# A decoder layer with expert retrieval: fewer v rows in the first chunk's stage, a shorter slot table for the next front

## The reference

```
h = x + W_out[concat(RMSNorm(SBAttn(q, k, v)), ConformerConv(c))]   # [q|k|v|c] = RMSNorm(x) W_in
y = h + PEER(RMSNorm(h))

def peer(xc):                      # one chunk of 128 tokens
    qh = xc @ wq                   # 8 heads, two half keys of 64
    v1, i1 = top_k(qh[..:64] . k1, 16);  v2, i2 = top_k(qh[..64:] . k2, 16)
    cand = v1[:, None] + v2[None, :];    top_s, pos = top_k(cand, 16)
    experts = (i1 * 128 + i2)[pos];      gates = softmax(top_s)
    act = gelu(u_tab[experts] . xc)
    return sum(gates * act * v_tab[experts])
```

## Time and profile before

| | |
|---|---|
| runs | 2912.07 us median, 2910.17 to 2914.2 |
| the profiled execution | span 2910.3 us |
| PE, matmuls | 2591.2 us (89%) |
| DVE | 2110.6 us (73%) |
| POOL | 1986.1 us (68%) |
| ACT | 871.6 us (30%) |
| moved by DMA | 1125 MB, mean 387 GB/s |
| gathers of phase 1 issued | from 337.11 us on |
| first gather of chunk 1 | 572.11 us |

### The profile page before, as it was taken

One profiled execution on the slowest core, in us unless ns is written; L12 is line 12 of the kernel. 1 busy time (PEld: TensorE's weight loads), 2 busy tenths in 40 slices (PEclk: granted clock), 3 DMA queues, 4 the chain that ended last, 5 costly groups with the idle time before them and its releaser, 6 DMA issues.

```text
span 2910.3 us, 29785 instructions
## 1 busy us (share of the span) xinstructions
PE 2591.2 (89%) x7585; PEld 1173.6 (40%) x7585; DVE 2110.6 (73%) x5267; ACT 871.6 (30%) x2022; POOL 1986.1 (68%) x2061
## 2 busy tenths in 40 slices
PE   8999979889978899799979999799988999777777
PEld 4544434433523444244523444244523445222222
DVE  5789758866887678777887778777787757744444
ACT  3223232243213421253214521264214631211111
POOL 1026566677777777777777777777777777777775
PEclk9999999999999999999999999999999999999999
DMA  6239899899999999999999999999999999999999
GB/s 239 96 127 382 331 416 369 316 402 414 419 419 419 413 419 419 409 414 409 416 416 406 411 419 419 419 392 413 419 419 399 385 419 419 415 420 419 420 419 364
DMA packets 321344, 1125.04 MB, mean 387 GB/s; under 512 B 35937, under 2 KB 43641, under 8 KB 321176
## 3 DMA queue, kind: packets, MB, share of 16 engines
q0 software_dynamic: 294912, 1073.87, 91.7%
q1 hardware_dynamic: 26264, 49.27, 4.8%
HBM read 1114.62 MB, written 8.39 MB: 386 GB/s over the span
## 4 chain that ended last, share of the span: by engine, by line
PE 41%; DMA 25%; issue 16%; POOL 12%; DVE 4%; ACT 2%; POOLq 0%; SPq 0%; ACTq 0%; DVEq 0%
PE psum L1614 21%; DMA w_kept<-in_peer_u,experts 12%; DMA ring_v<-in_peer_v,experts 10%; PE psum L514 9%; POOL w_kept L1517 7%; POOL ring_v L1517 5%; PE psum L1038 3%; PE psum L1064 3%; PE psum L1548 2%; DVE w_kept L1933 1%; PE psum L1574 1%; DMA w_kept<-in_peer_v,experts 1%; PE psum L1564 1%; DMA qT_spill<-qT_out 1%; ACT L1751 0%
## 5 line engine op out<-in xcount | busy, mean ns | idle before, releaser
L1614 PE MATMUL psum<-ring_v,diag 128*128 128x512 f32 x3364 | 1619.6, 607 | 252.6 <-DMA ring_v<-in_peer_v,experts 163.9
L1933 DVE CUSTOM_DVE_ANT_0 w_kept<-w_kept,psum 128x1024 f32<-128x1024 f32 x928 | 1125.5, 1217 | 551.2 <-DMA w_kept<-in_peer_u,experts 548.1
L1517 POOL DMA_INDIRECT w_kept<-in_peer_u,experts x928 | 898.2, 968 | 300.1 <-issue 231.4
L1517 POOL DMA_INDIRECT ring_v<-in_peer_v,experts x878 | 847.8, 966 | 327.3 <-issue 234.5
L1614 PEld LDWEIGHTS psum<-ring_v,diag 128*128 128x128 f32 x3364 | 587.1, 191 | 1058.8 <-issue 775.2
L1760 ACT ACTIVATE diag<-ident,weights 128x128 f32<-128x128 f32 x981 | 354.2, 393 | 746.9 <-PE psum L1614 589.9
L1614 PE MATMUL psum<-w_kept,diag 128*128 128x512 f32 x560 | 269.9, 604 | 37.3 <-DMA w_kept<-in_peer_v,experts 23.5
L514 PE MATMUL psum<-w_sb,xnT 128*128 128x512 f32 x640 | 283.5, 599 | 0.8 <-ACT xnT L679 0.8
L466 POOL DMA_INDIRECT w_kept<-in_peer_u,experts x96 | 90.2, 940 | 236.7 <-DVE experts L1324 184.9
L1889 DVE SCALAR_TENSOR_TENSOR acc<-conv_in,taps,acc 128x128 f32<-128x128 f32 x720 | 205.0, 346 | 0.2
L514 PEld LDWEIGHTS psum<-w_sb,xnT 128*128 128x128 f32 x640 | 120.6, 192 | 143.4 <-issue 137.7
(11 more groups left out here) (230 smaller groups left out, 1750.9 us busy)
## 6 DMA issues: line engine op xcount, KB each, us to landing
w_kept<-in_peer_u,experts POOLq DMA_INDIRECT x1024, 9.5
ring_v<-in_peer_v,experts POOLq DMA_INDIRECT x878, 9.5
w_sb<-in_w_in SPq DMA_DIRECT2D x4, 2048.0 KB, 17.6
x_in<-in_x SPq DMA_DIRECT2D x8, 512.0 KB, 6.3
w_kept<-in_w_out SPq DMA_DIRECT2D x1, 4096.0 KB, 14.8
h_res<-in_x SPq DMA_DIRECT2D x8, 512.0 KB, 6.8
w_kept<-in_peer_wq SPq DMA_DIRECT2D x2, 2048.0 KB, 10.6
wo_sb<-in_w_out SPq DMA_DIRECT2D x1, 4096.0 KB, 19.9
```

The source lines that it names most:

```text
L1517: nc.gpsimd.indirect_dma_start(slot(kind, n), None, peer_u[0] if kind == "u" else peer_v[0], bass.IndirectOffsetOnAxis(S.experts[c % 2][:, ...
L1614: last = nc.tensor.matmul(y_ps[:, j * BANK:(j + 1) * BANK], diag[:, e % DIAGS, :], slot("v", n)[:, j * BANK:(j + 1) * BANK], start=e == 0, ...
L1933: nc.vector.tensor_tensor_reduce(out=row, in0=row, in1=hn, scale=1.0, scalar=0.0, op0=ALU.mult, op1=ALU.add, accum_out=dots[:, e:e + 1]).t ...
```

## The change

A class `Plan` computes the front's table from five numbers. Chunks 2 to 7 keep the old table (`LONG`). Chunk 1's front, which runs beside chunk 0's rows, gets a shorter one (`SHORT`): a head every 3 slots, mix in 8, query in 9, the search one slot a step, two of the best-steps in a slot. It comes to 87 slots (`FIRST_SLOTS`), numbered 0 to 86, and chunk 0's stage has that many. In front slots: attention to 29, mix 35 to 42, residual to transposes 43 to 47, query 49 to 57, scores 56, 57, 60, 61, search 58 to 67, candidates 68 to 70, best 71 to 75, look-up 77 to 84, experts 85, gates 86.

v rows get a table of their own, `v_slot`. Chunk 0: 80 rows (`FIRST_ROWS`) from slot 4 on, nearly one a slot, and the 48 others in slots 0 to 47 of chunk 1's stage. Chunk 1's v rows lie evenly from slot 48 of its stage to slot 27 of chunk 2's (128 rows in 108 slots, so that some slots have two), chunk 2's from 28 to slot 19 of chunk 3's (120 slots), and from chunk 3 on it is as before. The stages of chunks 1 to 7 keep 128 slots. `add_h` goes to 2 and 4 slots behind the lag (6 and 8 in chunk 0, 50 and 52 in chunk 1), and `copy_y` / `end_first_y` to the lag. Diagonals are made 3 slots ahead of their row, as before. Of chunk 0's 80 rows every sixth goes aside, 13 instead of 36.

Chunk 0's sum stays in `y_side` and is stored from there. SP's order: the loads of q and conv of chunk f + 1 stand behind the residual's of f, in chunk 1's stage ahead of the store. The diff, cut to its core (each engine's `front` reads the same table; `front_slot` takes the stage's own number of slots):

```diff
-SPREAD = TOPK + 1
-ADD_H = (LAG + 4, LAG + 8)
+BUILD = 3
+FIRST_ROWS = 80
+LAGS = {0: 4, 1: ROWS - FIRST_ROWS, 2: 28}
...
+class Plan:
+    def __init__(self, att_step, mix_slots, query_slots, search_step, per_best):
+        self.step = att_step
+        self.att_end = end = att_step * (HEADS - 1) + ATT_USE
...
+        self.mix, self.mix_slots = end + 6, mix_slots
+        self.h_add, self.h_mean, self.h_norm, self.h_t = (self.mix + mix_slots + n for n in (0, 1, 3, 4))
+        self.query, self.query_slots = self.h_t + 2, query_slots
...
+        first = self.score[1] + 1
+        second = max(self.score[3] + 1, first + (5 if search_step == 1 else 1))
+        self.search = tuple(first + search_step * n for n in range(5)) + tuple(second + search_step * n for n in range(5))
...
+SHORT, LONG = Plan(3, 8, 9, 1, 2), Plan(5, 16, 18, 2, 1)
+FIRST_SLOTS = SHORT.slots
...
+def plan(f):
+    return SHORT if f == 1 else LONG
+
+def slots_of(c):
+    return FIRST_SLOTS if c == 0 else SLOTS
...
-    CAUGHT = ROWS - LAG
-    first_at = {4 + e * (SLOTS - 5) // CAUGHT: e for e in range(CAUGHT)}
-    SIDE = ([row_of(FIRST, e) for e in range(CAUGHT) if e % 3 == 2]
+    STARTS = [sum(slots_of(n) for n in range(c)) for c in range(CHUNKS + 1)]
+    v_slot = []
+    for c in range(CHUNKS):
+        begin, end = STARTS[c] + lag(c), STARTS[c + 1] + lag(c + 1)
+        v_slot += [begin + e * (end - begin) // ROWS for e in range(ROWS)]
+    v_slot[0:ROWS] = [4 + e * (STARTS[1] - 5) // FIRST_ROWS for e in range(FIRST_ROWS)] + [
+        STARTS[1] + n for n in range(ROWS - FIRST_ROWS)]
...
+    SIDE = ([row_of(FIRST, e) for e in range(FIRST_ROWS) if e % 6 == 5]
             + [row_of(TAIL, e) for e in range(ROWS - LAG, ROWS) if e % 3 == 0])
...
+        def load_queries(f):
+            sp.wait_ge(S.z_ready, UNITS * f)
+            sp.dma_start(qT[:, :, :].rearrange("p b t -> p (b t)"), qT_spill[f]).then_inc(S.q_in, 16)
+            sp.wait_ge(S.tapped, TAP_OPS * f)
+            sp.dma_start(conv_in[:, :, :], hT_spill[:, :, f * P:f * P + HALO + P]).then_inc(S.c_in, 16)
...
         def step(c, f):
+            if c is None:
+                return
+            late_rows = lag(c) > LAG + TOPK
+            if late_rows and f is not None and f + 1 < CHUNKS:
+                load_queries(f + 1)
+            if later(c):
+                store(c - 1)
             if f is not None:
-                load_front(f)
-            if c is not None and later(c):
-                store(c - 1)
+                load_residual(f)
+                if not late_rows and f + 1 < CHUNKS:
+                    load_queries(f + 1)
...
-            for s in range(SLOTS):
-                u, v = u_at(c, s), v_at(c, s)
+            for s in range(slots_of(c)):
+                u = u_at(c, s)
                 if u is not None:
                     gather("u", c, u)
-                if v is not None:
+                for v in v_at(c, s):
                     gather("v", *v)
...
-                    if s in ADD_H:
-                        add_h(c, ADD_H.index(s))
+                    for j in range(2):
+                        if s == lag(c) + 2 + 2 * j:
+                            add_h(c, j)
...
-                    if s == LAG and c > FIRST + 1:
+                    if s == lag(c) and c > FIRST + 1:
                         copy_y(c - 1)
...
             if later(f):
                 dve.wait_ge(S.taken, f)
                 dve.wait_ge(S.h_T, 2 * f)
+            if f > 2:
                 dve.wait_ge(y_stored, 16 * (f - 1))
...
+            if n == FIRST_SIDES:
+                dve.wait_ge(y_stored, 16)
...
-            dve.wait_ge(S.taken, FIRST + 2)
...
-                nc.vector.tensor_tensor(y_out[:, at], y_ps[:, at], y_side[:, at], ALU.add).then_inc(y_copied, 1)
+                nc.vector.tensor_tensor(y_side[:, at], y_ps[:, at], y_side[:, at], ALU.add).then_inc(y_copied, 1)
```

More of the change, by code:

```diff
@@ L73 @@
[L73 to L75 removed]
 LOOKS = 8
[L77 to L79 removed]
+MIX_STEPS, QUERY_STEPS = 16, 18
 EARLY_TAPS = range(TAPS - OWN_TAPS)
[L81 to L82 removed]
+class Plan:
+    def __init__(self, att_step, mix_slots, query_slots, search_step, per_best):
+        self.step = att_step
+        self.att_end = end = att_step * (HEADS - 1) + ATT_USE
+        self.conv_t, self.ln_stat, self.ln_scale, self.conv_back = (end + n for n in (-1, 0, 2, 3))
+        self.o_mean, self.o_norm, self.o_t = (end + n for n in (1, 2, 3))
+        self.mix, self.mix_slots = end + 6, mix_slots
+        self.h_add, self.h_mean, self.h_norm, self.h_t = (self.mix + mix_slots + n for n in (0, 1, 3, 4))
+        self.query, self.query_slots = self.h_t + 2, query_slots
+        self.queried = (self.query + (query_slots + 1) // 2 + 1, self.query + query_slots + 1)
+        self.score = (self.queried[0] + 1, self.queried[0] + 2, self.queried[1] + 1, self.queried[1] + 2)
+        first = self.score[1] + 1
+        second = max(self.score[3] + 1, first + (5 if search_step == 1 else 1))
+        self.search = tuple(first + search_step * n for n in range(5)) + tuple(second + search_step * n for n in range(5))
+        self.cand = self.search[-1] + 1
+        self.best = tuple(self.cand + 3 + n // per_best for n in range(10))
+        self.shift = self.split = self.best[-1] + 1
+        self.look = self.split + 1
+        self.experts = self.look + LOOKS
+        self.gates = self.experts + 1
+        self.slots = self.gates + 1
+        self.tap_slots = ([end + 5 + n * (first - end - 5) // len(EARLY_TAPS) for n in EARLY_TAPS]
+                          + [ATT_SUM + 2 + att_step * n for n in range(OWN_TAPS)])
+        assert len(self.tap_slots) == TAPS and self.tap_slots[-1] < self.conv_t
@@ L619, in query_first @@
         def query_first():
-            for n in range(QUERY_SLOTS):
-                query(0, n)
+            for n in range(QUERY_STEPS):
+                query(0, n, QUERY_STEPS)
             score_keys(0, 0)
@@ L635, in _ @@
         transpose_qk(1)
-        for n in range(MIX_SLOTS):
-            mix(0, n)
+        for n in range(MIX_STEPS):
+            mix(0, n, MIX_STEPS)
         project(2, A)
@@ L1035, in mix @@
         total = 2 * KT_D
-        for m in range(total * n // MIX_SLOTS, total * (n + 1) // MIX_SLOTS):
+        for m in range(total * n // steps, total * (n + 1) // steps):
             j, k = m // KT_D, m % KT_D
@@ L1059, in query @@
         total = PH * KT_D
-        for m in range(total * n // QUERY_SLOTS, total * (n + 1) // QUERY_SLOTS):
+        for m in range(total * n // steps, total * (n + 1) // steps):
             h, k = m // KT_D, m % KT_D
@@ L1653, in front_slot @@
             elif f + 1 < CHUNKS:
-                front(f + 1, s + LEAD - SLOTS)
+                front(f + 1, s + LEAD - slots)
         def step(c, f):
-            for s in range(SLOTS):
+            for s in range(SLOTS if c is None else slots_of(c)):
                 if c is not None:
-                    v = v_at(c, s)
-                    if v is not None and not in_side(*v):
-                        add_row(*v)
-                    if s in ADD_H:
-                        add_h(c, ADD_H.index(s))
+                    for v in v_at(c, s):
+                        if not in_side(*v):
+                            add_row(*v)
+                    for j in range(2):
+                        if s == lag(c) + 2 + 2 * j:
+                            add_h(c, j)
                 front_slot(f, s)
@@ L1812, in front_slot @@
             elif f + 1 < CHUNKS:
-                front(f + 1, s + LEAD - SLOTS)
+                front(f + 1, s + LEAD - slots)
         def step(c, f):
-            for s in range(SLOTS):
+            slots = SLOTS if c is None else slots_of(c)
+            for s in range(slots):
                 if c is not None:
@@ L1837, in _ @@
         gelu(CHUNKS - 1, PH - 1)
-        for e in range(ROWS - SPREAD, ROWS):
+        for e in range(ROWS - (LAG - BUILD), ROWS):
             if not in_side(TAIL, e):
```

174 lines of the change are left out of this document (79 added, 95 removed).

## The result

The changed kernel takes 2922.08 us (median of six runs, 2919.07 to 2922.98), the kernel before in the same comparison 2912.23 us (six runs, 2910.17 to 2914.66). The ratio is 1.0029, with a 95% interval from 1.0019 to 1.0039: 9.9 us slower. The forecast was 2921. The profiled execution has a span of 2917.1 us; its own time, 2919.07, is the lowest of the six.

What follows compares the result with a forecast made beforehand. Bound: POOL's gather pace of 1.242 us behind chunk 0's stage; within it transfers early, later PE, then DVE. Moved gathers cost 34.8 us, the earlier first gather returns 26.1: 2912.1 + 8.7 = 2921 us, range 2908 to 2936.

Steps and rivals of the forecast that it cites:

- The pace behind chunk 0's stage: 28 gathers moved behind chunk 1's first gather cost 1.242 us each on POOL, 34.8 us more there.
- few us: Sign of being wrong: the stages from chunk 3 on differ from before by more than this.
- Slot 28: Second half of mix's first slot in chunk 0's stage: reached near 424 us, against 421 by the transfers alone.
- The PE stream to the search: PE in chunk 0's stage, mix to scoring: 65.4 us of work and 1 us of waits, search from about 490.5.
- DVE's tail: DVE from first search to experts: 40.1 us search, six dot rows, five side rows, 1.2 us waits; 54.3 us, experts 544.8.
- First gather: POOL's first gather of chunk 1, ending chunk 0's stage: at 546 us instead of 572.1, with 112 gathers ahead.
- no-change rival: PE fills its early waits, slot 28 at 420, tail without waits, first gather 539: loss 1.7 us, 2914; chance 0.26.
- Chunks 1 and 2: Their stages: about 271 gathers in some 346 us and 268, no POOL waits; PE's 23 extra rows cost nothing.
- The sum: 34.8 us lost behind chunk 1's first gather less 26.1 us gained before it: +8.7 us, 2921.
- The port rule: VectorE instructions with two SBUF inputs lengthen POOL's gathers; fewer side rows free at most 14 us, costed at nothing.

Runs made afterwards that it cites:

- half_gather: The changed kernel with the 143 v gathers of chunk 1's stage bringing 512 of 1,024 columns; 2917.41 us, ratio 1.0017.
- rows_only_2: The changed kernel with its v row places and thinned side rows, but the old long table and 128 slots; 2919.50 us, ratio 1.0025.
- early_sides_2: The changed kernel with every third of rows 0 to 45 aside (15) instead of every sixth of 80 (13); 2910.46 us, 0.9991; on the first chip 3312.36 us.
- table_only_2: The changed kernel with its short table and 87 slots, but chunk 0's 108 rows and every third aside as before; 2913.35 us, ratio 1.0003.
- balanced: The kernel before with 41 side rows for 36, every second up to row 63 and every fifth behind; 2911.34 us, ratio 0.9993.
- balanced_short: The changed kernel with 108 rows in chunk 0's stage, 39 aside, every second up to row 59, every fifth behind; 2906.92 us, ratio 0.9982.
- half_pe_2: The changed kernel, PE skipping the second half of the columns of chunk 0's rows 80 to 126 and chunk 1's 1 to 126; 2920.66 us, 1.0027.

## Why the prediction was right

- **The pace behind chunk 0's stage.** 28 gathers at 1.242 us were to cost 34.8 us; it is 32.8. The pace holds, and half_gather shows whose it is. Part of the 2.0 us is the scatter of single profiles: from chunk 1's first gather to the tail's the other two kernels with the moved rows take 2326.9 and 2327.2 us (rows_only_2, early_sides_2), those with 140 gathers in chunk 0's stage 2295.0, 2291.6, 2292.0 and 2293.7 (before, table_only_2, balanced, balanced_short). The means differ by 34.3 us. Chunk 1's stage has 17.3 us more for 15 gathers (18.6 at the pace) and chunk 2's 14.2 for 12 (14.9). Part of the difference is that gathers longer than 0.94 us cost 2.5 us in chunk 1's stage, for 8.3 before. The rest, 1.3 us more in the stages of chunks 3 to 6, is the sum of -1.8, +5.5, -1.5 and -0.9. The +5.5 of chunk 4's stage is more than the "few us" that I had named as a sign of being wrong, and it is no scatter: this stage takes 330.7 to 331.3 us in all five profiles with moved rows and 325.2, 326.5 and 327.8 in before, table_only_2 and balanced (330.2 in balanced_short). In the changed kernel gathers longer than 0.94 us cost 9.4 us in it, for 4.8 before. I had no term for that; over the stages 3 to 6 it nearly cancels.
- **Slot 28.** 424, measured 425.50. It was an estimate between two bounds, 421 by the transfers and 13 us more of PE work against some 10 us of waits, and right to 1.5 us.
- **The PE stream to the search.** 65.4 us of work and 1 us of waits from there to 490.5; measured 65.3 from 425.50 to 490.83. Part by part: mix and its rows 25.8 us (425.50 to 451.3) for 25.8; on to the transposes 8.8 for 9.5; from there to the search 30.8 for 2.6 + 26.3 + 1.2 and the 1 us of waits, 31.1.
- **DVE's tail.** 54.3 us, measured 53.2: six dots and five side rows stand in it as forecast, and the wait for data that I carried over (1.2 us) did not occur. Experts at 544.07 for 544.8.
- **First gather.** 545.94 for 546, with 112 ahead. It is held as forecast by the last v gathers, which wait for DVE's side rows: behind the wait that ends at 535.63 (side row 65, slot 70) POOL issues eight gathers without a pause. That it is right to 0.1 us is luck in part: slot 28 came 1.5 us late, the stream to the search and the tail together 2.2 us short, and the way from the experts to the gather 0.7 us long. The no-change rival (539) was right on the tail (53.1) and fell on slot 28, 425.50 for its 420.
- **Chunks 1 and 2.** 344.7 us for 271 gathers and 343.0 for 268, where 346 was forecast for the first. Waits of POOL beyond the 0.30 us are 6.2 and 4.2 us, 1.5 and 5.3 before: not none, as I wrote, but half_pe_2 shows that they aren't a price of PE's work, since with half of it they are 5.2 and 7.1. The 23 rows given back to PE were rightly costed at nothing.
- **The sum.** +8.7 us, profiled spans +6.8, medians +9.9. The terms give the 6.8 (32.8 - 26.2 + 0.2); that the medians lie 1.2 us from the forecast, and not 3 or 4, owes something to chance.
- **The port rule.** It was costed at nothing, and the gathers of chunk 0's stage that ran long did become fewer. Beside a side row 3 of 12 gathers took over 1.1 us from 392 to 545, where it had been 14 of 47, but in that stretch POOL was waiting in any case, 16.0 us for side rows alone (above), so the rule changed nothing in this change. The Trainium skill, SBUF — State Buffer, section Who interferes with whom, says that a VectorE instruction with two SBUF inputs contends with a GpSimd instruction that reads SBUF; the counts under balanced agree, for side rows, for L1280 and for the dots with an input in PSUM, and there the price is not nothing: over all gathers from 392 to 560 us the time beyond 0.94 us sums to 10.3 us in the kernel before and to 17.4 in balanced.

What I had wrong were two later theories. The first, that table and rows are worth something only together: the term was "slots bring the search forward", and in table_only_2 most of the 9.8 us that it came forward went into dots that now lay behind it, and the rest into the v gathers left over. The second, in balanced, took each row off PE as 1.72 us gained, though from 392 to 450 us the transfers hold that part (share 1.03 in both kernels) and no row can be added sooner than it lands.

What the change loses on, put in one line: of each gather taken out of chunk 0's stage it gets back 26.2 / 28 = 0.94 us and pays 1.17 us (32.8 / 28) behind it, or 1.22 by the means above. The moved rows free PE of few instructions (67 rows for 72, as 23 side rows went back to PE), and up to the first search DVE waits for PE (11.62 us); behind it, POOL waits for the side rows in DVE's search. That side rows which all stand early (15 for 13) make up the loss is shown by early_sides_2; other numbers and places were not tried.

## What to carry to other kernels

When work is moved out of a stage into one that is bound by a fixed pace, compare what each moved piece gives back at its old place with that pace, on the engine that the old place waits for. A shorter table of slots, with every third row aside as before, gave nothing here, because it took no instructions away from that engine; ask which instructions lie between the start and the result that the next stage waits for, and whether an engine that works in order still has other work queued ahead of the use of that result, as POOL's last v gathers here. Where the last waiter is an engine with work of its own in the tail, move that work ahead of the tail first. Check a named releaser against the code: the buffer's last user, not the name in the profile, told here that POOL waited for DVE.

## What the runs showed of the hardware

On the first chip the gathers went slower; each chip was used in one session only, so whether it is the chip, the time or what else ran beside it can't be told. Groups on POOL over 250 us of a late stage, early_sides on the first chip from 3000 us on, and the kernel before on its chip from 2600 us on:

```profile
L1561 POOL DMA_INDIRECT w_kept<-in_peer_u,experts x87 | 81.8, 940 | 26.5 <-issue 24.7 <-DVE dots L1982 0.9 <-remote 0.6
L1561 POOL DMA_INDIRECT ring_v<-in_peer_v,experts x75 | 70.5, 940 | 55.7 <-issue 22.4 <-PE psum L1658 17.1 <-remote 10.8
```
```profile
L1517 POOL DMA_INDIRECT w_kept<-in_peer_u,experts x101 | 94.7, 938 | 30.8 <-issue 28.1 <-DVE dots L1933 2.7
L1517 POOL DMA_INDIRECT ring_v<-in_peer_v,experts x87 | 81.5, 937 | 26.5 <-issue 20.4 <-DVE dots L1933 6.1
```

The instruction takes the same 0.94 us, yet 174 gathers (with 12 into w_kept for v) stand in 250 us for 202, 1.44 us each for 1.24: there POOL waits for ring buffers, and the profile's page gives a mean of 340 GB/s for 387. PE is busy for 182 and DVE for 108 of those 250 us, so neither holds: on that chip the transfers are the bound. On the others it is POOL's issuing: half of the bytes of 143 gathers brought 0.9 us there. The other surprise is that halving PE's work in a stage lowered its clock: in half_pe_2 the busy time fell from 314.6 to 249.4 us while the granted clock fell from 1.00 to 0.85, a mean between the two levels of 1.2 and 2.4 GHz, and the passes over ring_v took 760 ns in the mean for 603. PE had been idle more: in this stage it waited 86 us for v rows, for 20 in the changed kernel.
